# A top-k search whose second half runs on one fp32 key, and an attention whose exponentials run a slot later and whose scales are fetched a batch later

## The reference, cut to what matters

```python
# sparse mixer: every query keeps its 256 best admissible keys
score = einsum('bqh,bqhs->bqs', iw, relu(einsum('bqhd,bsd->bhqs', iq, ik)))
score = where(adm, score, -inf)
_, idx = lax.top_k(score, 256)        # ties go to the lower index
gathered_attention(q, k, v, idx, valid)

# forgetting attention: causal, with a bias per head and key
s = qk * scale + cumf_q - cumf_k
softmax(where(causal, s, -inf)) @ v
```

## Time and profile before

| | us |
|---|---|
| three runs | 1698.61, 1703.37, 1703.47 (median 1703.37) |
| the profiled execution | 1698.1, of which the span 1696.3 |
| projection with the search | 0 to 354.7 |
| fox | 354.7 to 555.4 |
| dsa | 555.4 to about 745 |
| mix_out and ffn | about 745 to 1696.3 |
| TensorE busy | 1497.9 (88%) |
| VectorE busy | 836.1 (49%) |
| ScalarE busy | 572.6 (34%) |
| GpSimd busy | 417.9 (25%) |

### The profile page before, as it was taken

One profiled execution on the slowest core, in us unless ns is written; L12 is line 12 of the kernel. 1 busy time (PEld: TensorE's weight loads), 2 busy tenths in 40 slices (PEclk: granted clock), 3 DMA queues, 4 the chain that ended last, 5 costly groups with the idle time before them and its releaser, 6 DMA issues. The chain is left out here.

```text
span 1696.3 us, 21939 instructions
## 1 busy us (share of the span) xinstructions
PE 1497.9 (88%) x8492; PEld 1312.0 (77%) x8492; DVE 836.1 (49%) x1616; ACT 572.6 (34%) x1042; POOL 417.9 (25%) x431
## 2 busy tenths in 40 slices
PE   6999899828788487869979999999999999999985
PEld 6879899816566365648859898998989989899873
DVE  3379999866674577844771212212122131221338
ACT  3467788216564377741022011110111101011100
POOL 3413334401221012213313221122211222112216
PEclk9999999959999699989989999999999999999997
DMA  6102213057651401141122011010110101112002
GB/s 202 44 7 73 78 59 101 1 120 150 164 142 28 127 20 38 33 143 56 41 75 75 26 52 67 30 49 25 50 64 34 49 25 50 62 37 74 0 0 103
DMA packets 80040, 109.08 MB, mean 64 GB/s; under 512 B 14824, under 2 KB 61640, under 8 KB 79968
## 3 DMA queue, kind: packets, MB, share of 16 engines
q1 hardware_dynamic: 79968, 108.14, 21.3%
HBM read 85.82 MB, written 12.33 MB: 58 GB/s over the span
## 5 line engine op out<-in xcount | busy, mean ns | idle before, releaser
L2124 DVE TENSOR_TENSOR rows<-rows,down 128x512 f32<-128x512 f32 (+1 forms) x198 | 135.0, 685 | 215.3 <-PE down L1979 215.3
L2108 DVE TENSOR_TENSOR prod<-gated,up 128x1056 f32<-128x1056 f32 x22 | 27.6, 1254 | 334.8 <-PE up L1934 334.8
L1934 PE MATMUL gate<-h_hi,gu_hi 128*128 128x352 f32 x528 | 171.0, 324 | 0.6 <-POOL gu_lo L2058 0.6
L1979 PE MATMUL down<-down_hi,act_hi 128*128 128x512 f32 (+1 forms) x396 | 159.5, 403 | 12.4 <-DVE rows L2124 8.6
L1934 PE MATMUL up<-h_hi,gu_hi 128*128 128x352 f32 x528 | 170.3, 323 | 0.0
L1934 PE MATMUL gate<-h_lo,gu_hi 128*128 128x352 f32 x528 | 169.3, 321 | 0.0
L1934 PE MATMUL up<-h_lo,gu_hi 128*128 128x352 f32 x528 | 169.2, 321 | 0.0
L1934 PE MATMUL up<-h_hi,gu_lo 128*128 128x352 f32 x528 | 169.1, 320 | 0.0
L1934 PE MATMUL gate<-h_hi,gu_lo 128*128 128x352 f32 x528 | 169.1, 320 | 0.0
L1979 PE MATMUL down<-down_lo,act_hi 128*128 128x512 f32 (+1 forms) x396 | 158.2, 400 | 0.0
L1979 PE MATMUL down<-down_hi,act_lo 128*128 128x512 f32 (+1 forms) x396 | 158.1, 399 | 0.0
(11 more groups left out here) (324 smaller groups left out, 3684.7 us busy)
## 6 DMA issues: line engine op xcount, KB each, us to landing
gate_raw<-in_w_gate SPq DMA_DIRECT2D x11, 1024.0 KB, 5.3
up_raw<-in_w_up SPq DMA_DIRECT2D x11, 1024.0 KB, 5.4
down_raw<-in_w_down SPq DMA_DIRECT2D x11, 1024.0 KB, 7.4
w_raw<-in_w_in SPq DMA_DIRECT2D x9, 1024.0 KB, 5.6
x_raw<-in_xT SPq DMA_DIRECT2D x8, 528.0 KB, 8.3
key_bias<-scratch_negc SPq DMA_DIRECT2D x8, 512.0 KB, 4.7
fox_scales<-scale_rows SPq DMA_DIRECT2D x16, 256.0 KB, 3.7
dsa_scales<-scale_rows SPq DMA_DIRECT2D x16, 256.0 KB, 3.2
```

The lines of the kernel that those rows point to most:

```text
L1934: mm = nc.tensor.matmul(bank[:, ch, 0:TC], l, r, start=(k == 0 and i == 0), stop=(k == KD - 1 and i == 2))
L1979: mm = nc.tensor.matmul(pd[0:rows, i % 2, :], l, r, start=n == 0, stop=n == 5)
L2108: nc.vector.tensor_tensor(prod[:, :].rearrange("p (c r) -> p c r", c=NCH), gated[:, :].rearrange("p (c r) -> p c r", c=NCH), pu[:, :, 0:TC ...
L2124: nc.vector.tensor_tensor(o, o, pd[0:rows, i % 2, :], ALU.add).then_inc(added, 1)
```

## The change

It has four parts.

- **Second search on one key.** After the first search ACT writes (upper half minus the one found) times 65536 as fp32 into a buffer, segment by segment (`above`), and DVE adds the lower half and writes the sum over the segment (`key`). Two buffers alternate, so ACT's third activation waits for DVE's first addition. The second search counts on this fp32 key. The `limit` counts, `still`, the zeroing L831 and L837 go.
- **Ties.** After the second search ACT writes the sign of (low - key) of each segment over the segment as bf16 with its sum (`side`, seven activations, units evacuated between them). DVE has five passes per segment in place of seven, of which one is a single column. The wait for `w_lo_done` stands ahead of the scan of segment 3 only.
- **Attention.** ACT's exponentials of a slot run behind `hi` of the next slot; ahead of a batch's first step they are flushed. SP loads the scales of batch b-1 after the reciprocals of batch b.
- **fox loads.** The key bias of head i+2 is loaded in `loads` of batch 2i rather than 2i+1; the scan for `negc` comes first on DVE, and the first key biases no longer wait for the store of `bias_s`.

```diff
             act.wait_ge(planes_done, NSEG)
-            for p, plane in enumerate((hi_plane, lo_plane)):
+            for p, plane in enumerate((hi_plane, key)):
...
-                for part in range(2):
-                    act.wait_ge(limit_set[part], p + 1)
-                    for j in ON_ACT[part]:
-                        count(plane, j, limit, upto)
-                    evacuate((p * (BITS + 1) + BITS) * 2 + part)
+                if p == 0:
+                    act.wait_ge(top_set, 1)
+                    for i, j in enumerate(MASKED):
+                        if i >= 2:
+                            act.wait_ge(rest_done, i - 1)
+                        col = slice(COL[j], COL[j] + 1)
+                        nc.scalar.activation(above(j), hi_plane(j), ACT.Identity, scale=65536.0,
+                                             bias=top_value[0:SEG[j][2], col]).then_inc(above_done, 1)
+                        if i in (2, 5):
+                            evacuate(2 * BITS + i // 4)
+            act.wait_ge(low_set, 2)
+            for j in range(NSEG):
+                rows = SEG[j][2]
+                nc.scalar.activation(side(j), key(j), ACT.Sign, scale=-1.0, bias=low[0:rows, COL[j]:COL[j] + 1],
+                                     accum_out=sides[0:rows, j:j + 1]).then_inc(side_done, 1)
+                evacuate((2 * BITS + 1) * 2 + j // 2)
...
             for i, j in enumerate(MASKED):
-                nc.vector.scalar_tensor_tensor(lo_plane(j), hi_plane(j), one(j, top_key), lo_plane(j),
-                                               ALU.is_equal, ALU.mult).then_inc(act_masked, 1)
-            still(0, hi_plane, top_key)
+                dve.wait_ge(above_done, i + 1)
+                nc.vector.tensor_tensor(key(j), above(j), lo_plane(j), ALU.add).then_inc(rest_done, 1)
...
                         if s == 0:
                             if j >= 2:
-                                dve.wait_ge(step, n[0] - i)
-                            did(nc.vector.tensor_scalar(e, lo_plane(j), lo, None, ALU.is_equal))
+                                dve.wait_ge(step, n[0] - 1 - i)
+                            did(nc.vector.tensor_scalar(e, side(j), 0.0, None, ALU.is_equal))
                             continue
                         dve.wait_ge(step, n[0] - (len(pair) - 1))
                         if s == 1:
-                            did(nc.vector.scalar_tensor_tensor(e, hi_plane(j), top, e, ALU.is_equal, ALU.mult))
+                            if j == 3:
+                                dve.wait_ge(w_lo_done, NG)
+                            did(nc.vector.tensor_tensor_scan(r, e, e, 0.0, ALU.add, ALU.bypass))
                         elif s == 2:
-                            did(nc.vector.tensor_tensor_scan(r, e, e, 0.0, ALU.add, ALU.bypass))
+                            did(nc.vector.scalar_tensor_tensor(w, r[:, L - 1:L], 0.5, most[0:rows, j:j + 1], ALU.mult,
+                                                               ALU.add))
                         elif s == 3:
-                            did(nc.vector.scalar_tensor_tensor(e, r, w, e, ALU.is_le, ALU.mult))
-                        elif s == 4:
-                            did(nc.vector.scalar_tensor_tensor(e, lo_plane(j), lo, e, ALU.is_gt, ALU.add))
-                        elif s == 5:
-                            did(nc.vector.scalar_tensor_tensor(e, hi_plane(j), top, e, ALU.is_gt, ALU.add))
+                            did(nc.vector.scalar_tensor_tensor(e, r, w, side(j), ALU.is_le, ALU.subtract))
                         else:
-                            _, at, rows, L = SEG[j]
-                            did(nc.vector.tensor_scalar(score[0:rows, at:at + L], e, BIG, -BIG, ALU.mult, ALU.add))
+                            did(nc.vector.tensor_scalar(key(j), e, 0.0, -BIG, ALU.is_le, ALU.mult))
...
         for batch in batches:
+            if batch.sample:
+                if not batches[batch.b - 1].sample:
+                    load_scales(batches[batch.b - 1])
+                loads(sp, batch.b)
+                continue
             loads(sp, batch.b)
-            if batch.sample:
-                continue
             sp.wait_ge(recip_done, batch.b + 1)
+            if batch.b:
+                load_scales(batches[batch.b - 1])
             sp.dma_start(c["scale_rows"][batch.b].rearrange("(q i) -> q i", i=BH), rinv[:, batch.b % 4, :])\
                 .then_inc(scales_stored, 16)
...
+        waiting = []
         for slot in slots:
+            if slot.step is None or slot.step.part == 0:
+                for it in waiting:
+                    exp(it)
+                waiting = []
...
             if slot.step:
                 hi(slot.step)
-            for it in slot.logits:
+            for it in waiting:
                 exp(it)
+            waiting = list(slot.logits)
...
-            if b % 2 and b // 2 + 2 < FOX_H:
+            if b % 2 == 0 and b // 2 + 2 < FOX_H:
                 biased(b // 2)
                 load_bias(sp, b // 2 + 2)
+            if b == 4:
+                sp.wait_ge(bias_stored, 32)
```

More of the change, by code:

```diff
@@ L197, in project @@
         iT_new = b("iT_new", [P, 3, NEW], F32)
+        above_buf = Places(nc, half, rest)("above_top", [P, KEYS_S], F32)
         b = Places(nc, half, rest)
@@ L264, in lo_plane, with key, above, side @@
             return score[0:rows, at:at + L].bitcast(U16)[:, L:2 * L]
+        def key(j):
+            _, at, rows, L = SEG[j]
+            return score[0:rows, at:at + L]
+        def above(j):
+            buf = key_buf[:, :].bitcast(F32) if MASKED.index(j) % 2 else above_buf[:, :]
+            return buf[0:SEG[j][2], 0:SEG[j][3]]
+        def side(j):
+            _, at, rows, L = SEG[j]
+            return score[0:rows, at:at + L].bitcast(BF16)[:, 0:L]
         def flags(i, j):
@@ L791, in search @@
                 for part in range(2):
[L792 removed]
+                    cols = SETS[part]
                     dve.wait_ge(aim[part], aims(p, BITS))
[L794 to L802 removed]
+                    if p == 0:
+                        did(nc.vector.tensor_tensor(top_key[:, cols], candidate[:, cols], offset[:, cols], ALU.add))
+                    else:
+                        nc.vector.tensor_tensor(low[:, cols], candidate[:, cols], offset[:, cols], ALU.add)\
+                            .then_inc(low_set, 1)
             def aim_first(lowest):
@@ L812, in _ @@
             did(nc.vector.memset(cnt[:, :], 0.0))
-            did(nc.vector.memset(upto[:, :], 0.0))
+            did(nc.vector.memset(sides[:, :], 0.0))
+            for j in range(NSEG):
+                did(nc.vector.memset(konst[:, j:j + 1], TOPK - SEG[j][3] / 2))
             did(nc.vector.memset(offset[:, :], 0.0))
@@ L840, in _ @@
-            settled()
-            still(1, lo_plane, low)
-            dve.wait_ge(act_counted, counts_by(1, BITS, 1))
-            settled()
-            did(nc.vector.tensor_tensor(want[:, :], upto[:, :], allowed[:, :], ALU.subtract))
-            settled()
-            dve.wait_ge(w_lo_done, NG)
-            dve.wait_ge(act_counted, counts_by(1, BITS, 1))
-            for part in range(2):
-                acts = ACT_COLS[part]
-                did(nc.vector.tensor_scalar(want[:, acts], want[:, acts], 0.5, None, ALU.mult))
@@ L851, in _ @@
-            settled()
+            dve.wait_ge(low_set, 2)
             for j0 in range(0, NSEG, 2):
                 pair = range(j0, min(NSEG, j0 + 2))
-                for s in range(7):
+                last = pair[-1]
+                dve.wait_ge(side_done, last + 1)
+                did(nc.vector.scalar_tensor_tensor(most[:, j0:last + 1], sides[:, j0:last + 1], 0.5,
+                                                   konst[:, j0:last + 1], ALU.mult, ALU.add))
+                for s in range(5):
@@ L1039, in _, with load_scales @@
     def _(sp):
-        for batch in batches:
-            loads(sp, batch.b)
-            if batch.sample:
-                continue
-            sp.wait_ge(recip_done, batch.b + 1)
-            sp.dma_start(c["scale_rows"][batch.b].rearrange("(q i) -> q i", i=BH), rinv[:, batch.b % 4, :])\
-                .then_inc(scales_stored, 16)
+        def load_scales(batch):
             sp.wait_ge(scales_stored, 16 * (batch.b + 1))
@@ L1400, in pe_first @@
             mm.then_inc(lfT_done, 1)
[L1401 to L1402 removed]
+            pe.wait_ge(c_done, 2)
         def dve_first(dve):
```

74 lines of the change are left out of this document (35 added, 39 removed).

## The result

The changed kernel takes 1656.7 us (median of four runs, 1654.6 to 1661.6) beside 1703.4 for the kernel before on the same chip: a ratio of 0.9733 with a 95% interval of 0.9701 to 0.9765. The forecast was 1659 with 1641 to 1678. The total is right. Of the terms behind it that of dsa is too small, one of fox is right for the wrong reason, and those of fox depend on each other, where the sum takes them one by one.

The account below looks back on a forecast made before the run. DVE's tie loop was taken to bound the projection's end, engines waiting for each other fox. Projection -22.7, fox -11.1, dsa -6 sum to -39.8; from 1698.1 that gives 1658.3, with one for the runs' median 1659; range 1641 to 1678.

Parts of the forecast that it names:

- that of dsa: dsa: ACT's order takes 6 us of PE's waits for DVE's minimum, bounds +1 and -10.
- The projection: Projection: shorter search gap and tie loop start fox at 332.0 instead of 354.7, 22.7 us gained, bounds 17 to 24.
- T + 15.5: Projection: POOL ends the last weights 15.5 us after T, the end of the second search; DVE waits for them.
- PE's tail is last: Projection's end: PE's last units and POOL's last piece finish at 331.4, with 5.5 us of cover over DVE's 326.
- The rival of counts at twice the price: Second search: 64 DVE counts on fp32 take twice as long, 58 us more, 1716 in all; chance 0.06.
- fox, ACT's order: fox: exponentials a slot later save 2.05 us a head over seven heads and 1.5 in head 0, 15.8 together.
- fox, the key biases: fox: key biases of heads 3 and 5 issued some 5 us earlier, so PE waits of 9.1 us go.
- fox, the new stalls: fox: late scales delay POOL's values, PE stands 5.5 and 7.5 us; 14.2 lost with a late bias.
- The values of heads 2 and 4: fox: without samples' loads in between, the chain of bias, scales and POOL takes 21.4 us and just fits.
- the 1 to 2 us for a late key bias at head 4: fox: besides the stalls for values, 1 to 2 us more at head 4 for a bias now late.
- part of its wait for ACT's tail: fox: with the high part done first, part of DVE's wait for ACT's tail goes, within 2.05 us a head.
- the scales are hidden: fox: rival that POOL's values come in time and the two long stalls go, 1645 us; chance 0.20.

Follow-up runs that it names:

- tail_plus_9: Changed kernel with nine more DVE passes of 1024 four-byte elements behind the tie loop; 1657.5 us, ratio 0.9722.
- lag_alone: Changed kernel with key biases loaded at odd batches and exponentials in their own slot, both as before; scales still a batch behind; 1671.0 us, ratio 0.9831.
- scales_as_before: Changed kernel with the scales loaded in their own batch as before, key biases left at even batches; 1652.6 us, ratio 0.9725.
- bias_at_odd: Changed kernel with the key biases loaded at odd batches again, as before; 1641.2 us, ratio 0.9635.
- attention_alone: Kernel before with only the changed attention, behind the old projection; 1676.2 us, ratio 0.9845.
- scales_between: Changed kernel with SP issuing scales and store ahead of the wait for the last item's bias, next key bias and samples' loads; 1646.1 us, ratio 0.9646.
- past_batch_later: Changed kernel with the samples' past keys, biases and first values loaded at batches 5 and 9 instead of 4 and 8; 1645.7 us, ratio 0.9654.

## Why the prediction was right, and where it wasn't

**The projection** was right by its own steps. Forecast and found: first count of the second search at 208.7 and 209.1; fp32 counts of 1008 and 1007 ns; the scan of segment 3 waiting for the last weights until 303.4 (T + 15.5, T = 287.9) and 303.5; DVE done at 326 and 327.1; fox at 332.0 and 331.9. That PE's tail is last, with a few us of cover, is shown by tail_plus_9; the cover is 4.3 and not 5.5, because DVE ended 1.1 later. The rival of counts at twice the price is out by the row, 1007 ns at either width.

**fox, ACT's order: right in kind and in a head, a little too large in sum.** 2.15 us a head for 2.05, and 13.5 over the stage for 15.8, where the lag is in place and the key biases are not moved. The 2.3 us between are no more than the scatter of fox. The worth depends on the company: without the lag ACT's order brings 3.5 (200.9 to 197.4), in the change 7.9 (201.3 to 193.4), because key biases or values hold the faster heads up. The sum treated the 15.8 as independent of them.

**fox, the key biases: right number, wrong cause.** The step that failed reads "The key biases of heads 3 and 5 are issued some 5 us earlier, so the 9 us of PE waits go", which I gave to the move to even batches. lag_alone shows the 9.8 us with the key biases at odd batches. They come early because SP no longer waits for the store to land and for POOL before it goes on. I had costed the lag only for what it does to the scales, and of its effect on everything queued behind the removed waits I took nothing. The move then brings nothing that the lag hasn't brought: with ACT's new order the key bias of head 3 is issued 56.26 and 56.28 us into fox. Without the lag the move does bring something, 7.4 us, but not all of it: in scales_as_before PE still waits 3.96 and 6.02 us. That the number came out right, 9.8 for 9.1, is luck.

**fox, the new stalls: right in place and cause.** The values of heads 3 and 5 are late, 4.18 and 5.35 us on PE, where 5.5 and 7.5 were forecast. The values of heads 2 and 4, which were to fit, cost 1.69 and 0.94; the 1 to 2 us for a late key bias at head 4 didn't come. The landing was sized well: from the issue of the key bias the scales took 10.9 and 12.1 us (406.64 to 417.53 and 445.13 to 457.21) where issue and landing were to take 10.8 and 12.8, and POOL then took 3.5 for 3.6. But PE wanted the values 10.3 us behind that issue in both heads (416.93 and 455.45), where the forecast had 21.1 - 11.7 = 9.4. Besides, the prediction's own terms give 26.1 and 28.1 us, where it wrote 26.5 and 29. Together PE waits 12.2 us for 14.2, and the stage is 193.4 - 177.6 = 15.8 longer, which the scatter of fox doesn't tell from 14.2. PE's busy time differs too. The same 825 products take 148.5 us in the changed kernel and 141.8 in bias_at_odd, whose windows by stage are:

```profile
332.86:510.41 177.55, 141.80 (x825) 108.97 (x825) 117.19 (x285) 109.11 (x251) 39.79 (x32) 0.90 0.58 144
510.41:686.64 176.23, 138.00 (x756) 106.53 (x757) 126.87 (x295) 119.33 (x267) 31.39 (x37) 0.89 0.21 55
```

The product behind the stall at 421.11 took 0.80 us, where the earlier trace rows has 0.48 for such a product, and in the 12 us from 421 on the granted clock was 0.73: part of the price of a stall can come after it. How large a part isn't shown. In attention_alone 12.3 us of the same waits go with 145.5 us of busy PE, in scales_between no such wait with 144.7. As a sum along these runs: 200.9 - 9.8 - 13.5 + 15.8 = 193.4, which closes by construction. Against the 201.3 of before the forecast for fox was 3.2 us too good, again within two or three microseconds of scatter.

**dsa: the term was too small by half.** I took 6 of the 15 us of PE's waits for the minimum and gave -10 as the bound. Between executions whose clock at the end of dsa is alike it is 12.5 (193.4 in lag_alone, 180.9 in the change, 0.75 and 0.74 in the last 24 us) or 13.7 (189.9 before, 176.2 in bias_at_odd, 0.93 and 0.98). The 9.0 of the two profiles compares unlike ones. The bound of -10 was passed. Of PE's waits of the earlier trace rows, 11.6 and 7.2, the changed kernel has these:

```profile
PE dsa_transposed L1087 <- DVE dsa_nmax L1237: 5.7, 7, 1.5
PE dsa_logits L1654 <- DVE dsa_nmax L1237: 5.3, 7, 1.3
```

So 7.8 us went there, more than the 6 I took. Another group of waits I had never put in the sum, DVE's waits for ACT's tail in dsa. In lag_alone, with ACT's old order, and in the changed kernel they are:

```profile
DVE mixT L1263 <- ACT mixT L1178: 13.4, 11, 2.1
```
```profile
DVE mixT L1261 <- ACT mixT L1178: 6.1, 8, 2.1
```

For fox I had named them ("part of its wait for ACT's tail"), for dsa I left them out. How much of these 7.3 us reaches PE beside the 7.8 was not measured by itself.

**The sum.** In the profiled executions 39.6 us were gained, 39.8 forecast. The terms that missed went both ways, 3.2 too much in fox and 3.0 too little in dsa, so the total is better than its parts: its closeness is luck. With the shorter length of dsa the same profile would have gained some 44. By medians the gain is 46.7, since the executions that were profiled lay at the low end before (1698.1, beside 1698.6 to 1705.9 for the others) and on the upper side after (1658.5 of 1654.6 to 1661.6). The rival "the scales are hidden", at 1645, names the state of scales_between and past_batch_later (1646.1 and 1645.7): its price was right, it was not what the change does. One slip in the chances: half of 0.06 and 0.02 more make 0.05 for the same time and 0.03 for slower, where the prediction has 0.04 for each.

## What to carry over

A wait taken out of a queue that issues everything in order speeds up all that stands behind it: before giving a gain to a moved instruction, ask when it would be issued if it had stayed. Where a change takes a wait out and also moves work to be ahead of another wait, time the one without the other; here the lag was worth 9.8 us alone, and on top of it the move cost 10.2 with ACT's old order and 15.8 with the new one, though without the lag it gained 7.4. Two edits, each of which shortens what the other leaves in charge, can give less alone (in fox 3.5 and 9.8) than together (23.3), so that the sum of single trials is no bound. And a stage's length from one execution can be off by more than the effect in question.

## What the runs showed of the hardware

**The end of dsa has two lengths.** With ACT's new order it took 176.0 to 176.3 us in six kernels and 180.9 to 181.5 in four; with the old order 189.9 before and 193.4 to 193.7 in three. The same code for it took 176.1 in attention_alone, 180.9 in the change and 176.3 in tail_plus_9. The last 24 us of dsa in bias_at_odd, in the changed kernel and in lag_alone:

```profile
662.64:686.64 24.00, 18.47 (x99) 12.55 (x99) 9.39 (x25) 8.85 (x20) 3.44 (x5) 0.98 0.07 22
```
```profile
682.23:706.23 24.00, 18.48 (x85) 14.61 (x84) 8.13 (x21) 7.33 (x15) 3.45 (x5) 0.74 0.08 22
```
```profile
693.46:717.46 24.00, 18.48 (x86) 14.61 (x84) 8.14 (x21) 7.34 (x15) 3.45 (x5) 0.75 0.07 22
```

PE is busy for the same 18.5 us in each, but at a granted clock of 0.98 it does 99 products in that time and at 0.74 only 85. PE was well used in the stretch ahead (14.1 of 16 us in bias_at_odd, 14.5 in the changed kernel and in lag_alone, all at full clock), so the rows don't say what decides it; the difference of some 5 us is as large as what several of the experiments were to measure, and they had to be read by stage.

**A DVE pass without an accumulator is faster than a count.** Nine multiplications of 128x1024 four-byte elements took 7.75 us with their handovers, 0.86 each, where a count takes 1.14 for 896 of either width. The price of 1.1 that I expected of them was that of the count. The row of a price has to be of the same operation. The Trainium skill ("VectorE: DVE Perf Modes", section "The perf-mode tier table") has a scalar operation at four elements a cycle on 16 bits and two on fp32; its table has no row for one whose results are also summed. The counts, 1007 ns for 768 at both widths, don't follow it; of the multiplications the trace shows that they are quicker per element than a count.
